# Dense SwiGLU layer of a Trainium2 kernel: gate and up with the features on the partitions from the second block on

## The reference, cut to what matters

```
def rmsnorm(x, g):
    y = xf * lax.rsqrt(jnp.mean(xf * xf, axis=-1, keepdims=True) + EPS)
    return (y * g).astype(x.dtype)

def swiglu(h, wg, wu, wd):
    return (jax.nn.silu(h @ wg) * (h @ wu)) @ wd
...
hn = rmsnorm(h, ffn_norm[i])
h = h + swiglu(hn, dense_w_gate[j], dense_w_up[j], dense_w_down[j])   # 1024 -> 2816 -> 1024
```

## Time and profile before

| what | value |
|---|---|
| median of 3 runs | 1425.72 us (1425.20 to 1426.39) |
| profiled execution, its own time | 1425.05 us |
| its span, first to last instruction | 1423.2 us |
| busy: TensorE / VectorE / ScalarE | 99% / 81% / 66% of the span |
| granted clock of TensorE, mean | 0.996 |
| dense layer in the trace, second block on | about 147 to 316 us |

### The profile page before, as it was taken

One profiled execution on the slowest core, in us unless ns is written; L12 is line 12 of the kernel. 1 busy time (PEld: TensorE's weight loads), 2 busy tenths in 40 slices (PEclk: granted clock), 3 DMA queues, 4 the chain that ended last, 5 costly groups with the idle time before them and its releaser, 6 DMA issues.

```text
span 1423.2 us, 18448 instructions
## 1 busy us (share of the span) xinstructions
PE 1403.7 (99%) x6924; PEld 1163.1 (82%) x6925; DVE 1149.1 (81%) x1059; ACT 945.2 (66%) x880; POOL 84.6 (6%) x65
## 2 busy tenths in 40 slices
PE   8999999999999999999999999999999999999997
PEld 6888888887988888888888888888888888888885
DVE  5757654466577998898998998988899899898997
ACT  4645444445735777777777777777777777777775
POOL 1130000001122000000000000000000000000200
PEclk9999999999999999999999999999999999999999
DMA  8425555552334999999999999999999999999992
GB/s 338 172 90 194 204 195 179 194 218 89 149 139 171 339 386 364 385 380 376 379 390 381 371 388 387 361 383 382 370 382 389 382 370 393 385 364 369 420 403 107
DMA packets 63184, 438.20 MB, mean 308 GB/s; under 512 B 7199, under 2 KB 7377, under 8 KB 11906
## 3 DMA queue, kind: packets, MB, share of 16 engines
q1 hardware_dynamic: 59042, 423.27, 77.7%
q0 software_dynamic: 4064, 13.84, 2.5%
HBM read 430.79 MB, written 6.29 MB: 307 GB/s over the span
## 4 chain that ended last, share of the span: by engine, by line
PE 95%; DVE 3%; ACT 1%; issue 1%; DMA 1%; SPq 0%; DVEq 0%; ACTq 0%
PE ps L1763 50%; PE ps L1787 26%; PE ps L1514 3%; PE ps L1499 3%; PE ps L1600 3%; PE ps L1476 2%; PE ps L1779 2%; DVE w_lo L328 1%; PE ps L1823 1%; PE ps L1590 1%; DMA raw<-in_stream 1%; PE ps L1536 0%; DVE big L1066 0%; PE ps L1912 0%; PE ps L1546 0%
## 5 line engine op out<-in xcount | busy, mean ns | idle before, releaser
L328 DVE TENSOR_TENSOR w_lo<-raw,w_hi 128x2048 fp32r<-128x2048 f32 x399 | 919.7, 2308 | 169.1 <-ACT w_hi L323 167.8
L323 ACT ACTIVATE w_hi<-raw 128x2048 fp32r<-128x2048 f32 x399 | 764.0, 1916 | 214.0 <-PE ps L1787 109.2
L1763 PE MATMUL ps<-w_hi,xT_hi 128*128 128x512 f32 x1040 | 411.1, 395 | 0.5 <-DVE xT_lo L1190 0.5
L1763 PE MATMUL ps<-w_lo,xT_hi 128*128 128x512 f32 x1040 | 405.5, 390 | 0.0
L1763 PE MATMUL ps<-w_hi,xT_lo 128*128 128x512 f32 x1040 | 404.8, 389 | 0.0
L1763 PEld LDWEIGHTS ps<-w_lo,xT_hi 128*128 128x128 f32 x1040 | 195.2, 188 | 41.6
L1763 PEld LDWEIGHTS ps<-w_hi,xT_hi 128*128 128x128 f32 x1040 | 195.4, 188 | 39.8 <-DVE xT_lo L1190 0.7
L1763 PEld LDWEIGHTS ps<-w_hi,xT_lo 128*128 128x128 f32 x1040 | 195.5, 188 | 38.7
L1787 PE MATMUL ps<-w_hi,aT_hi 128*128 128x512 f32 x524 | 206.0, 393 | 0.0
L1787 PE MATMUL ps<-w_lo,aT_hi 128*128 128x512 f32 x524 | 204.4, 390 | 0.0
L1787 PE MATMUL ps<-w_hi,aT_lo 128*128 128x512 f32 x524 | 204.0, 389 | 0.0
(11 more groups left out here) (303 smaller groups left out, 1115.9 us busy)
## 6 DMA issues: line engine op xcount, KB each, us to landing
raw<-in_stream SPq DMA_DIRECT2D x400, 1024.0 KB, 7.2
outs<-work POOLq DMA_DIRECT2D x7, 512.0 KB, 9.0
gain<-in_gains POOLq DMA_DIRECT2D x4, 512.0 KB, 5.3
h<-in_x SPq DMA_DIRECT2D x2, 512.0 KB, 6.9
raw<-in_stream SPq DMA_DIRECT2D x2, 512.0 KB, 6.4
tokens<-big POOLq DMA_DIRECT2D x2, 512.0 KB, 3.0
out<-work SPq DMA_DIRECT2D x4, 256.0 KB, 2.6
cst<-in_consts SPq DMA_DIRECT2D x1, 581.0 KB, 11.0
```

The lines of the kernel that those rows point to most:

```text
L323: nc.scalar.activation(home(n, 0), raw[:, n % RAW, :], ACT.Copy).then_inc(hi_done, 1)
L328: nc.vector.tensor_tensor(home(n, 1), raw[:, n % RAW, :], home(n, 0).bitcast(F32), ALU.subtract).then_inc(lo_done, 1)
L1763: last = nc.tensor.matmul(ps[:, 4 + s, :], (xT_hi, xT_lo)[xp][:, k, x * P:(x + 1) * P], w((n + half), wp, kk * 512, (kk + 1) * 512), start ...
```

## The change

Block 0 stays as it was, except that its transposes go to bank 0. From block 1 on (`sides`) each matmul has a 128x128 piece of weights as the stationary operand and 256 tokens as the moving one. A side is 128 of the block's 256 features: its gate in columns 0 to 255 of a bank, its up in columns 256 to 511. Even blocks use banks 4 and 5, odd blocks 6 and 7, and no wait for `fd.mul` stands ahead of them. The result has the features on the partitions, so there are no transposes of activations behind it. The roots now lie along the columns: VectorE writes two diagonal matrices (`root_rows`), TensorE multiplies them by a matrix of ones, ScalarE copies the row to SBUF (`root_row`). VectorE multiplies gate and up by that row (`sides_scaled`), ScalarE applies Silu (`silu_sides`), VectorE multiplies both (`sides_mul`), ScalarE copies to the hi part (`sides_hi`) and VectorE takes the rest (`sides_lo`), all from SBUF. The loops over blocks are written out on the three engines. The splits of the first two units of the next mixer move: on VectorE the first stands behind the last side, the second between the residual and `rms` of token tile 0.

```diff
 # ScalarE
+            def silu_sides(b, sides=(0, 1)):
+                for f in sides:
+                    act.wait_ge(gate_scaled, 2 * (b - 1) + f + 1)
+                    nc.scalar.activation(gate_x[:, f, :], gate_x[:, f, :], ACT.Silu).then_inc(fd.silu, 1)
+            def sides_hi(b, dst, sides=(0, 1)):
+                for f in sides:
+                    act.wait_ge(fd.mul, 2 * b + f + 1)
+                    copy(dst[:, f, :, :], act_x[:, f, :].rearrange("p (t q) -> p t q", t=TT)).then_inc(fd.aT_hi, 1)
...
+            for b in range(1, DENSE_BLOCKS):
+                m = n0 + 3 * b
+                hi_unit(act, m + 1)
+                if b == 1:
+                    ffn_aT(fd, 2, 0, 0)
+                    act.wait_ge(row_ps, 1)
+                    copy(root_row, ps[:, 1, 0:SEQ]).then_inc(row_cp, 1)
+                else:
+                    if b == DENSE_BLOCKS - 1:
+                        hi_unit(act, m + 2)
+                    used(act, m - 1)
+                    sides_hi(b - 1, aT_hi)
+                if b < DENSE_BLOCKS - 1:
+                    hi_unit(act, m + 2)
+                    silu_sides(b)
+                    hi_unit(act, m + 3)
             hi_unit(act, END_UNIT + 1)
-            last_block(m + 3)
+            for f in range(2):
+                silu_sides(DENSE_BLOCKS - 1, (f,))
+                sides_hi(DENSE_BLOCKS - 1, end_aT_hi, (f,))
+            hi_unit(act, END_UNIT + 2)
 # VectorE
                 if L == 1:
                     residual(2, 0, n0)
+                    lo_unit(dve, n0 + 1)
                     rms(2, 0)
...
+            def root_rows():
                 for t in range(TT):
+                    ins = nc.vector.tensor_scalar(root_diag[:, t, :], ident, rs[:, t:t + 1], None, ALU.mult)
+                ins.then_inc(diag_done, 1)
+            def sides_scaled(b, n, sides=(0, 1)):
+                if b == 1:
+                    dve.wait_ge(row_cp, 1)
+                dve.wait_ge(fd.aT_lo, 2 * b)
+                for f in sides:
+                    if f == 0:
+                        dve.wait_ge(fd.gu_first, b + 1)
+                    else:
+                        used(dve, n)
+                    bank = 4 + 2 * (b % 2) + f
+                    nc.vector.tensor_tensor(gate_x[:, f, :], ps[:, bank, 0:SEQ], root_row, ALU.mult).then_inc(gate_scaled, 1)
+                    nc.vector.tensor_tensor(act_x[:, f, :], ps[:, bank, SEQ:2 * SEQ], root_row, ALU.mult).then_inc(up_scaled, 1)
...
+            for b in range(1, DENSE_BLOCKS):
+                m = n0 + 3 * b
+                lo_unit(dve, m + 1)
+                if b == 1:
+                    ffn_aT(fd, 2, 0, 0)
+                else:
+                    if b == DENSE_BLOCKS - 1:
+                        lo_unit(dve, m + 2)
+                    sides_lo(b - 1, aT_lo, aT_hi)
+                if b < DENSE_BLOCKS - 1:
+                    lo_unit(dve, m + 2)
+                    sides_scaled(b, m + 1)
+                    sides_mul(b)
+                    lo_unit(dve, m + 3)
...
+            sides_scaled(b, END_UNIT - 1, (1,))
+            sides_mul(b, (1,))
+            sides_lo(b, end_aT_lo, end_aT_hi, (1,))
+            lo_unit(dve, END_UNIT + 1)
 # TensorE
+            def sides(b, n):
                 for half in range(2):
+                    unit_ready(n + half)
+                    for side in range(2):
                         for kk in range(4):
                             k = 4 * half + kk
+                            for f in (side, side + 2):
+                                for xp, wp in PASSES:
+                                    last = nc.tensor.matmul(ps[:, 4 + 2 * (b % 2) + side, f // 2 * SEQ:(f // 2 + 1) * SEQ],
+                                                            w(n + half, wp, kk * 512 + f * P, kk * 512 + (f + 1) * P),
+                                                            (xT_hi, xT_lo)[xp][:, k, :],
+                                                            start=(k == 0 and f < 2 and xp == wp),
+                                                            stop=(k == KT - 1 and wp == 1), skip_group_check=True)
...
+            def root_rows():
+                pe.wait_ge(diag_done, 1)
+                nc.tensor.matmul(ps[:, 1, 0:SEQ], ones, small[:, 0:SEQ], start=True, stop=True).then_inc(row_ps, 1)
...
+            def dense_end(n):
+                whole(sides(DENSE_BLOCKS - 1, n - 3))
                 unit_ready(n - 1)
-                pe.wait_ge(fd.aT_lo, B + 1)
-                down_tile(n - 1, 0, aT_hi[:, 0], aT_lo[:, 0], False, False)
+                pe.wait_ge(fd.aT_lo, 2 * (DENSE_BLOCKS - 1))
+                down_tile(n - 1, 0, aT_hi[:, :, 0], aT_lo[:, :, 0], False, False)
                 unit_ready(n)
-                pe.wait_ge(half_aT_lo, 1)
-                half_aT(1)
...
+                pe.wait_ge(fd.aT_lo, 2 * DENSE_BLOCKS)
+                down_tile(n, 0, end_aT_hi[:, :, 0], end_aT_lo[:, :, 0], False, True).then_inc(first_tile, 1)
+                down_tile(n - 1, 1, aT_hi[:, :, 1], aT_lo[:, :, 1], False, False).then_inc(unit_used, 1)
+                down_tile(n, 1, end_aT_hi[:, :, 1], end_aT_lo[:, :, 1], False, True, (0,))
...
+            for b in range(1, DENSE_BLOCKS - 1):
+                gu = sides(b, n0 + 3 * b - 1)
+                next(gu)
+                if b == 1:
+                    act_T(fd, 2, 0, 0)
+                    root_rows()
+                whole(gu)
+                dense_down(b - 1, n0 + 3 * b + 1)
             dense_end(n0 + DENSE_UNITS - 1)
```

More of the change, by code:

```diff
@@ L287, in build @@
         place_done, dense_root = sem("place_done"), sem("dense_root")
[L288 removed]
+        diag_done, row_ps, row_cp, gate_scaled, up_scaled = (
+            sem(n) for n in ("diag_done", "row_ps", "row_cp", "gate_scaled", "up_scaled"))
         half_tile, row_gain, row_root, row_ready = sem("half_tile"), sem("row_gain"), sem("row_root"), sem("row_ready")
@@ L1275, in _ @@
             ffn_block(fd, 2, 0, 0, n0 + 2)
+            root_rows()
             lo_unit(dve, n0 + 3)
[L1277 to L1295, removed]
+            for b in range(1, DENSE_BLOCKS):
[12 more added lines that the diff above has]
+                    lo_unit(dve, m + 3)
+            b = DENSE_BLOCKS - 1
+            sides_scaled(b, END_UNIT - 1, (0,))
+            sides_mul(b, (0,))
+            sides_lo(b, end_aT_lo, end_aT_hi, (0,))
+            sides_scaled(b, END_UNIT - 1, (1,))
+            sides_mul(b, (1,))
+            sides_lo(b, end_aT_lo, end_aT_hi, (1,))
+            lo_unit(dve, END_UNIT + 1)
             def root_of(t):
@@ L1813, in dense_end @@
                 for half in range(2):
[L1814 to L1817, removed]
+                    unit_ready(n + half)
+                    for side in range(2):
                         for kk in range(4):
                             k = 4 * half + kk
[L1820 to L1826, removed]
+                            for f in (side, side + 2):
[5 more added lines that the diff above has]
+                                                            stop=(k == KT - 1 and wp == 1), skip_group_check=True)
+                        if half == 1 and side == 0:
@@ L1827, in dense_end, with dense_down @@
                             last.then_inc(fd.gu_first, 1)
                     last.then_inc(unit_used, 1)
-                    if half == 0:
-                        act_T(fd, 2, B, 1)
+                    yield
+            def root_rows():
+                pe.wait_ge(diag_done, 1)
+                nc.tensor.matmul(ps[:, 1, 0:SEQ], ones, small[:, 0:SEQ], start=True, stop=True).then_inc(row_ps, 1)
+            def dense_down(b, n):
+                unit_ready(n)
+                pe.wait_ge(fd.aT_lo, 2 * (b + 1))
+                if b == 0:
+                    pe.wait_ge(row_cp, 1)
+                for t in range(TT):
+                    last = down_tile(n, t, aT_hi[:, t] if b == 0 else aT_hi[:, :, t], aT_lo[:, t] if b == 0 else aT_lo[:, :, t],
+                                     b == 0, False)
+                last.then_inc(unit_used, 1)
@@ L1872, in expert_end @@
                         last.then_inc(sc_ps if half else end_ps, 1)
[L1874 to L1882, removed]
             def token_ids(e):
```

62 lines of the change are left out of this document (17 added, 45 removed).

## The result

The changed kernel takes 1429.05 us (median of 15 runs, 1428.28 to 1430.02), the kernel before 1425.72 (15 runs, 1425.0 to 1426.58): ratio 1.0023, 95% interval 1.0017 to 1.0030, 3.33 us slower.

The account below looks back on a forecast made before the run. TensorE's own list of work was taken as the bound. +1.43 us up to the last gate/up matmul and +1.05 from there to the mixer gave +2.5: 1427.5 us profiled, 1428.2 median, range 1426.0 to 1430.3.

Parts of the forecast that it names:

- blocks 2 to 10: Nine dense-layer blocks, each losing four transposes: 11.47 us of matmuls against 11.36, +0.11 us a block, +1.0 together.
- block 1: First block with sides: slower pace +0.59 us, new f32 product of ones and root diagonals +0.21, a wait gone -0.14.
- the two transposes of the last gate/up: Block 10: two transposes ahead of the last gate/up matmuls go, -0.23 us.
- last gate/up to the mixer: From the last gate/up result drained to the mixer: late rms +1.34 us, two transposes gone -0.29, together +1.05.
- Columns of a matmul: Dense-layer gate/up: two 256-column matmuls at 119.5 ns replace one of 512 at 226.7, 5.9 us more over 480 pairs.
- VectorE and ScalarE in the middle: Middle blocks: VectorE's added work, 3.4 us where it had 1.65, is covered by 5.9 us of slack; costed at nothing.
- The end: Dense layer's end: the unit split between residual and rms delays rms, and so TensorE, by 1.34 us.
- The last activation chain: Five operations after T, when the last gate/up result is drained: done at T + 2.3, hidden by 0.2 us.
- The matmul of half the columns: Rival on gate/up matmuls: half the columns cost half, 113.4 ns or below, giving 1422.3 us; chance 0.07.
- The end does not cost nothing: Denies the rival that rms is late before the mixer but the delay is taken up, 1426.9 us; chance 0.08.
- The last chain did not miss its cover: Denies the rival of 1 us more in five last operations, TensorE waiting 0.8 before the second twelve, 1429.0; chance 0.06.
- TensorE was fed: Denies the rival that weight loads lag in the sides, one gap in each of 20 units, 6.8 us, 1435; chance 0.09.

Follow-up runs that it names:

- the three stacked kernels: Changed kernel with hi and lo tokens as 512 moving columns in blocks 1 to 9: 1428.02 us; plus a halved split 1427.25; plus adjacent SBUF placement 1427.30.
- the one of hi and lo side by side: Changed kernel with 512 moving columns in blocks 1 to 9, VectorE's split halved around the residual, hi and lo adjacent in SBUF: 1427.30 us.
- the kernel before with the late split: Kernel before, with only the split of the next mixer's second unit moved between residual and rms of token tile 0: 1427.18 us.

## Why the prediction was right, and what it had too small

The mechanism was right on both counts: the doubled number of matmuls costs a little more than the transposes, and the root of the next mixer came late. The terms, as forecast and as read in the profiled pair:

| term | forecast | measured |
|---|---|---|
| blocks 2 to 10 | +1.0 us | 9 x (16.98 - 16.80) = +1.62 |
| block 1 | +0.59 + 0.21 - 0.14 = +0.66 | 12.37 - 11.60 = +0.77 |
| the two transposes of the last gate/up | -0.23 | not separate; with the two rows above the layer grew by 2.15 |
| last gate/up to the mixer | +1.05 | 13.62 - 12.50 = +1.12 |
| sum | +2.5 | +3.3 |

*Columns of a matmul.* I took 119.5 ns from 22 intervals; 96 in a row show 119.9. That is 0.04 us a block, and the down unit behind them takes 5.47 us where it took 5.44 (first matmuls behind a change of width at 230 to 240 ns). 0.07 us against a net term of 0.11 is small, but it comes nine times, and it is the step that was too small: the difference of two large numbers, sized from a short run. The Trainium skill's isolated formula (TensorE: Matmul & The Clock Gate, section Back-to-back issue gap) would have put the kernel at 1423.5, as an estimate; the changed kernel's own stream, 119.9 ns against its 109.2, again does not agree with it.

*Block 1.* The f32 product costs 0.43 us, not 0.21: it runs in two records, and I had read the distance behind one of them.

*VectorE and ScalarE in the middle.* Costed at nothing, and more than two further microseconds of VectorE a block changed nothing.

*The end.* The moved split was costed at 1.34 and measured at 1.28 and 1.30 in two kernels. The last activation chain was forecast to be done at T + 2.3 and TensorE to come at T + 2.5; from the start of the scaling (312.17) it was 2.32 and 2.48. It is hidden by 0.16 us.

*The rivals.* The matmul of half the columns does not cost half: it takes 119.9 ns where half is 113.4, and at 192 columns still 111. The end does not cost nothing. The last chain did not miss its cover. TensorE was fed: 1184 matmuls in 165.20 us without an idle moment.

*What failed* is one sentence: behind the mixer's first matmul operations did not all keep their distance. In the profiled pair the terms above give 3.27 us up to the mixer. Ahead of them the trace of the changed kernel is 0.62 us earlier, so the mixer starts 2.64 later. Behind them the stretch up to the experts is 0.60 longer, the experts 0.34, and the way from the last matmul with weights to the end of the span 1.00. But for rounding that adds up to the 4.58. The first matmul of the experts, before and after:

```profile
457.92 0.50 PE L1763 MATMUL ps<-w_hi,xT_hi 128*128 128x512 f32 x1 [0.52 <-DVE xT_lo L1190]
```

```profile
461.16 0.50 PE L1794 MATMUL ps<-w_hi,xT_hi 128*128 128x512 f32 x1 [0.52 <-DVE xT_lo L1217]
```

The 0.60 us have a visible place, told in the last section. The earlier start and the later end are not chance of one execution, since they go with the kernel. The last matmul of block 0 starts at 146.9 to 147.1 us in the three traces with tokens on the partitions, and at 146.4 to 146.8 in the eight with sides as in the change. From TensorE's last matmul to the end pass 10.1 to 10.2 us in the former and 10.7 to 11.2 in the latter (the three stacked kernels have 147.2 to 147.3 and 10.5 to 10.6). No run says why. So it is partly luck that the medians' 3.33 us are so near the 3.27 of the terms: their interval, 2.4 to 4.3 us, leaves what lies outside of the terms open to about a microsecond either way, and the prediction had nothing there.

## What to carry to other kernels

When one layout has half as wide matmuls as the other, price the fixed part of each matmul (13 ns here at 128 stationary columns) before the work that the new layout saves: four transposes were worth 0.43 to 0.48 us a block, 48 more matmuls 0.63. A split or copy that is off the path belongs into an engine's idle time by size: 2.3 us put into a gap of 0.8 delayed everything behind it, while in two halves around the residual 0.8 of the 1.3 us that it cost hid. And where a forecast is a small difference of large sums, take the pace from the longest run that the trace has, and count the records of an f32 product.

## What the runs showed of the hardware

*A floor under narrow matmuls.* With a load of 128 stationary columns ahead of each, matmuls of 128, 192 and 256 moving columns (fp32r) follow one another at 111.1, 111.5 and 119.9 ns, and of 512 at 226.7.

*A stretch at 1.2 GHz with a place of its own.* All traces show TensorE granted its full clock through the dense layer and the second mixer, and then a stretch at half of it around the router, where TensorE had waited for VectorE. It lasts 6.8 us in thirteen of them and 10.2 in the one of hi and lo side by side. Windows of the kernel before, then of the changed one; PEclk is the third number from the right:

```profile
442.00:448.00 6.00, 5.74 (x41) 4.88 (x39) 5.21 (x11) 4.62 (x7) 2.32 (x2) 1.00 0.43 152
448.30:455.00 6.70, 6.60 (x31) 6.60 (x32) 4.92 (x25) 4.95 (x7) 1.35 (x3) 0.50 0.36 143
```

```profile
446.90:452.30 5.40, 4.74 (x37) 4.05 (x35) 4.50 (x16) 4.02 (x8) 2.90 (x2) 1.00 0.61 234
452.60:459.30 6.70, 6.43 (x29) 6.14 (x30) 5.18 (x18) 3.30 (x5) 1.06 (x2) 0.50 0.43 149
```

The mixer had moved by 2.64 us, the slow stretch by 4.3. So it lies over other work. Before, it caught the last logits: eight tiny matmuls at 0.21 us each. After, these ran at 0.11, and more of the token matmuls behind them was slow. In the traces the slow stretch begins 125.1 to 127.9 us behind the mixer's first matmul. Where it begins at 125.1 to 125.3 (three traces, the kernel before among them) a matmul of the experts comes 141.3 to 141.4 us behind the mixer's first; at 126.9 to 127.9 (nine traces, the changed kernel and the kernel before with the late split among them) the same takes 142.0 to 142.3, and the one at 125.8 takes 141.6. The trace with the longer stretch, from 126.4 on, takes 142.6. It looks as if a shift of what lies ahead moves the work against the slow stretch and so gives or takes 0.6 to 0.9 us, and up to 1.3 where the stretch is longer. That is nearly as much as the moved split cost, and it is read from traces only: no experiment set it by itself, and whether it goes the same way in each execution of one kernel stays open.
